# Conditioning loaded by column halves, with eight projection units moved into the second half's loading, in a one-core decoder-layer kernel

## What is computed

```python
mod = (jax.nn.silu(c) @ w_ada + b_ada)[:, None, :]
sh1, sc1, gt1, sh2, sc2, gt2 = jnp.split(mod, N_MOD, axis=-1)
h = rmsnorm(x, g_pre_mix) * (1.0 + sc1) + sh1
m, k_rows, v_rows, s_new = token_mixer(h, w_in, ...)      # proj = h @ w_in, attention, GLA, @ w_out
x = x + gt1 * rmsnorm(m, g_post_mix)
h = rmsnorm(x, g_pre_ffn) * (1.0 + sc2) + sh2
f = (jax.nn.silu(h @ w_ffn_gate) * (h @ w_ffn_up)) @ w_ffn_down
x = x + gt2 * rmsnorm(f, g_post_ffn)
```

## Time and profile before

| what | value |
|---|---|
| time, median of 3 runs | 1493.67 us (1493.54 to 1495.06) |
| profiled execution: time | 1496.05 us |
| profiled execution: span, first to last instruction | 1494.3 us |
| PE busy in the span | 1428.4 us (96%) |
| DVE, ACT busy | 921.6 us (62%), 665.5 us (45%) |
| chain that ended last | PE 83%, DMA 11%, DVE 2%, ACT 2% |
| read from and written to device memory | 382.28 MB, 11.34 MB |

### The profile page before, as it was taken

The page is one execution under the profiler, slowest core; times in us unless marked ns, Lnnn a source line. Parts: engine busy times, 40 slices in busy tenths (PEclk is TensorE's granted clock), DMA queues, the critical chain, the costliest instruction groups (busy, mean ns, idle before and its releaser), DMA issues.

```text
span 1494.3 us, 29193 instructions
## 1 busy us (share of the span) xinstructions
PE 1428.4 (96%) x11238; PEld 1273.0 (85%) x11238; DVE 921.6 (62%) x1519; ACT 665.5 (45%) x1303; POOL 103.8 (7%) x200
## 2 busy tenths in 40 slices
PE   6779999998899999998999999999999999999997
PEld 2247787887667777796899999999999999999997
DVE  2243588995777666368756766567665675446444
ACT  1023477777656454345543434434344343334333
POOL 0000311113322210000000000000000000200000
PEclk9979999999899999999999999999999999999999
DMA  9999999999999979985755565555655555855552
GB/s 370 422 343 364 390 391 405 374 352 391 396 370 343 340 255 356 409 307 225 250 182 183 170 193 173 181 182 170 191 174 181 182 170 192 231 181 181 181 178 95
DMA packets 139330, 396.82 MB, mean 266 GB/s; under 512 B 13162, under 2 KB 17681, under 8 KB 126433
## 3 DMA queue, kind: packets, MB, share of 16 engines
q1 hardware_dynamic: 118018, 319.66, 61.3%
q0 software_dynamic: 21232, 76.10, 13.4%
HBM read 382.28 MB, written 11.34 MB: 263 GB/s over the span
## 4 chain that ended last, share of the span: by engine, by line
PE 83%; DMA 11%; DVE 2%; ACT 2%; issue 1%; POOLq 0%; SPq 0%; POOL 0%; DVEq 0%; ACTq 0%
PE ps L1981 24%; PE ps L1982 24%; PE ps L1983 24%; DMA ada_s<-in_w_ada 5%; PE ps L1915 4%; DMA v_page<-in_cache_v 3%; PE ps L2113 2%; DMA ada_r<-in_w_ada 1%; PE ps L2039 1%; DMA raw<-in_w_ffn_gate 1%; DMA k_page<-in_cache_k 1%; ACT k_page L803 1%; DMA k_page<-in_cache_v 1%; ACT w_hi L715 0%; PE ps L2141 0%
## 5 line engine op out<-in xcount | busy, mean ns | idle before, releaser
L1981 PE MATMUL ps<-h_hi,w_hi 128*128 128x264 f32 x2304 | 667.8, 290 | 11.0 <-DVE h_lo L1249 3.6
L1982 PE MATMUL ps<-h_lo,w_hi 128*128 128x264 f32 x2304 | 659.2, 286 | 0.0
L1983 PE MATMUL ps<-h_hi,w_lo 128*128 128x264 f32 x2304 | 658.6, 286 | 0.0
L1981 PEld LDWEIGHTS ps<-h_hi,w_hi 128*128 128x128 f32 x2304 | 438.9, 190 | 55.8 <-issue 34.9
L1806 DVE TENSOR_TENSOR w_lo<-raw,w_hi 128x1024 fp32r<-128x1024 f32 x254 | 307.2, 1214 | 273.1 <-ACT w_hi L1047 271.7
L1047 ACT ACTIVATE w_hi<-raw 128x1024 fp32r<-128x1024 f32 x264 | 278.5, 1059 | 408.2 <-PE ps L1983 384.4
L1982 PEld LDWEIGHTS ps<-h_lo,w_hi 128*128 128x128 f32 x2304 | 438.2, 190 | 0.5
L1983 PEld LDWEIGHTS ps<-h_hi,w_lo 128*128 128x128 f32 x2304 | 436.9, 190 | 0.0
L1261 DVE TENSOR_TENSOR w_lo<-raw,w_hi 128x1024 fp32r<-128x1024 f32 x138 | 168.7, 1223 | 145.9 <-ACT w_hi L715 145.5
L715 ACT ACTIVATE w_hi<-raw 128x1024 fp32r<-128x1024 f32 x128 | 135.1, 1056 | 172.5 <-PE ps L1983 155.1
L1982 PE MATMUL ps<-act_lo,w_hi 128*128 (+1 forms) x704 | 200.4, 285 | 0.0
(11 more groups left out here) (362 smaller groups left out, 1213.8 us busy)
## 6 DMA issues: line engine op xcount, KB each, us to landing
ada_r<-in_w_ada SPq DMA_DIRECT2D x64, 1024.0 KB, 9.1
raw<-in_w_in SPq DMA_DIRECT2D x96, 512.0 KB, 8.3
raw<-in_w_ffn_gate SPq DMA_DIRECT2D x88, 512.0 KB, 3.5
raw<-in_w_ffn_up SPq DMA_DIRECT2D x88, 512.0 KB, 4.4
raw<-in_w_ffn_down SPq DMA_DIRECT2D x88, 512.0 KB, 4.6
ada_s<-in_w_ada SPq DMA_DIRECT2D x32, 1024.0 KB, 13.7
k_page<-in_cache_k POOLq DMA_DIRECT2D x64, 512.0 KB, 8.0
v_page<-in_cache_v POOLq DMA_DIRECT2D x38, 512.0 KB, 8.4
```

The lines of the kernel that those rows point to most:

```text
L1981: mm(out, w_hi, xh, start=first, stop=False)
L1982: mm(out, w_hi, xl, start=False, stop=False)
L1983: return mm(out, w_lo, xh, start=False, stop=last)
```

## The change

Three things change together.

1. **Columns by halves.** A first step now takes 1024 columns of the shift and the same 1024 of the scale (`ada_halves`), so 16 steps give both for channels 0 to 1023, and 16 more for the rest. `mod_part` and `samples` work on half of the channels.
2. **Units behind steps.** Groups 0 and 1 are cut in two. Their first four units each (the first eight in the order, `unit_of`) need only channels 0 to 1023 and run between the steps of the second half (`UNIT_BEHIND` on PE, `W_BEHIND` on SP). The other four units of each follow as slots 8 to 15; their sums are added by DVE to what ACT copied out (`evac_sum`). The slot programs start at slot 8 (`NSPLIT`).
3. **Steps moved.** n = 0 to 15 now stand in slots 9 to 32, 16 to 23 in slots 34 to 48 (even), and the second half of shift 2 (24 to 31) in slots 97 to 105, with a turn of its own; 32 to 47 in slots 108 to 123. n = 48, 49 and 54 are loaded at the FFN's start. POOL loads the first five K pages before it makes the tree masks. The gate's products move from slots 4, 6, 8 to slots 9, 11, 13.

```diff
-        PARTS = (1, 0, 2, 3, 4, 5)
-        TURN_BANK = (4, 7, 4, 4, 7, 4)
+        PARTS = (0, 0, 2, 3, 3, 4, 5)
+        TURN_BANK = (4, 7, 4, 4, 7, 7, 4)
+        PART_END = (0, 0, 16, 24, 32, 48, 64)
...
+        def unit_of(u):
+            if u < 2 * NSPLIT:
+                half, i = divmod(u, NSPLIT)
+                g, j = divmod(i, UPC // 2)
+                return g, j + half * UPC // 2
+            return divmod(u, UPC)
...
-        A_SLOT = {n: 3 + 9 * n // 8 for n in range(16)}
-        A_SLOT.update({16 + k: 25 + 2 * k for k in range(16)})
-        A_SLOT.update({32 + k: s for k, s in enumerate(
-            (96, 97, 98, 100, 101, 102, 103, 104, 105, 106, 107, 108, 110, 111, 112, 114))})
+        A_SLOT = dict(enumerate((9, 10, 12, 13, 14, 15, 16, 17, 19, 20, 22, 24, 26, 28, 30, 32)))
+        A_SLOT.update({16 + k: 34 + 2 * k for k in range(8)})
+        A_SLOT.update(dict(zip(range(24, 32), (97, 98, 100, 101, 102, 103, 104, 105))))
+        A_SLOT.update({32 + k: 108 + k for k in range(16)})
-        TURN_AT = {20: 2, 55: 3, 115: 4}
+        TURN_AT = {33: 2, 55: 3, 106: 4, 124: 5}
...
+            def ada_halves(n):
                 q, k = divmod(n, KC)
-                return ada_v[:, k, PARTS[q] * 2048:PARTS[q] * 2048 + 2048]
+                return ada_v[:, k, 0:2 * D].rearrange("p (c q i) -> p c q i", c=2, q=2)[:, :, q, :]
...
+            W_BEHIND = {16: 0, 17: 1, 19: 2, 20: 3, 22: 4, 23: 5, 25: 6, 26: 7, 29: 8, 30: 9}
             for n in range(6, 2 * KC):
                 sp.wait_ge(ads_used, n - 5)
-                sp.dma_start(ADS[n % 6][:, :], ada_start(n)).then_inc(ads_in[n % 6], 16)
-            for u in range(4):
-                w_load(u)
+                ada_first_load(n)
+                if n in W_BEHIND:
+                    u = W_BEHIND[n]
+                    if u >= 4:
+                        sp.wait_ge(lo_ready, u - 3)
+                    w_load(u)
...
             mod_row(0)
+            for i in range(3):
+                hi(i)
+                h_high(i)
+            for u in range(3, 7):
+                hi(u)
+            act.wait_ge(ads_used, 14)
+            for m in range(MT):
+                evac(0, m)
+            hi(7)
+            for m in range(MT):
+                evac(1, m)
+            hi(8)
+            hi(9)
             mod_row(1)
-            hi(0)
-            for i in range(NH):
-                h_high(i)
-                if i < 3:
-                    hi(i + 1)
+            h_high(3)
+            hi(10)
+            h_high(4)
...
             mod_part(0)
...
+            samples(0)
+            for i in range(3):
+                prompt(i)
+                lo(i)
+                low(i)
+            for u in range(3, 10):
+                lo(u)
             mod_part(1)
-            dve.wait_ge(mod_done, 2)
-            build_h(0)
+            samples(1)
+            prompt(3)
+            low(3)
+            prompt(4)
+            lo(10)
+            low(4)
+
+            def evac_sum(e, m):
+                if m < 3:
+                    dve.wait_ge(bank_done, 3 * e + m + 1)
+                else:
+                    dve.wait_ge(unit_used, SET_END[e])
+                dve.wait_ge(bank_out, MT * NG)
+                dst = unit_dst(e - NG, m)
+                v.tensor_tensor(dst, dst, ps[:, m, 0:T], ALU.add).then_inc(bank_out, 1)
...
+            UNIT_BEHIND = {18: 0, 19: 1, 20: 2, 22: 3, 23: 4, 25: 5, 26: 6, 28: 7}
+            for n in range(KC, 2 * KC):
+                ada_first(n)
+                if n == KC + 1:
+                    mod_turn(0)
+                if n in UNIT_BEHIND:
+                    unit(UNIT_BEHIND[n])
+            mod_turn(1)
```

More of the change, by code:

```diff
@@ L120, in stickbreak_gla_layer @@
         GLU = put("glu", [P, MT, T], at=r0 + 2 * FC * T * 4)
-        ADS = [put(f"ada_s{i}", [P, 2048], at=r0 + 8192 * i) for i in range(6)]
+        ADS = [put(f"ada_s{i}", [P, 2048], at=r0 + 8192 * i) for i in range(8)]
+        ADS_PLACE = [n % 6 if n < 18 or n % 6 >= 2 else 6 + n % 6 for n in range(2 * KC)]
         MNEG0 = put("mask_neg0", [P, P], at=r0 + 98688)
@@ new lines, in prompt, with low, samples @@
+            def prompt(i):
+                for k in range(*HPC[i]):
+                    ins = v.tensor_scalar(F_LO[:, k, 0:TP], F_LO[:, k, 0:TP], scale_t[:, k, 0:1], MOD[:, k, 0:1], ALU.mult, ALU.add)
+                ins.then_inc(h32_ready, 1)
+            def low(i):
+                cs = slice(*HPC[i])
+                dve.wait_ge(hhi_ready, i + 1)
+                v.tensor_tensor(H_LO[:, cs, :], F_LO[:, cs, :], H_HI[:, cs, :].bitcast(F32), ALU.subtract).then_inc(h_ready, 1)
+            def samples(q):
+                cs = slice(KC // 2 * q, KC // 2 * (q + 1))
+                dve.wait_ge(mod_done, q + 1)
+                link(v.scalar_tensor_tensor(scale_t[:, cs, :], MOD[:, KC + cs.start:KC + cs.stop, :], 1.0,
+                                            vec1[:, NMOD + cs.start:NMOD + cs.stop].unsqueeze(2).to_broadcast([P, KC // 2, NC]),
+                                            ALU.add, ALU.mult))
+                link(v.tensor_tensor(F_LO[:, cs, TP:T], F_LO[:, cs, TP:T], scale_t[:, cs, 1:NC], ALU.mult))
+                v.tensor_tensor(F_LO[:, cs, TP:T], F_LO[:, cs, TP:T], MOD[:, cs, 1:NC], ALU.add)
@@ L1684, in slot @@
                     fold(SQD[:, 12:16, :], MT, acc_ready)
+                if NG <= SET_AT.get(st, 0) < 2 * NG:
+                    for m in range(3):
+                        evac_sum(SET_AT[st], m)
             def gate_scales(gain, part):
@@ L1703, in fold @@
                 ins.then_inc(done, 1)
-            for st in range(NSLOT):
+            for st in range(NSPLIT, NSLOT):
                 slot(st)
@@ L1911, in _, with ada_step @@
             ins.then_inc(tr_done, 1)
-            def ada_step(ring, k, bank):
+            def ada_step(ring, k, bank, first, last):
                 for j in range(4):
-                    ins = mm(ps[32 * j:32 * j + 32, bank, :], CTK[:, k, :], ring[:, j * CG:(j + 1) * CG],
-                             start=(k == 0), stop=(k == KC - 1))
+                    ins = mm(ps[32 * j:32 * j + 32, bank, :], CTK[:, k, :], ring[:, j * CG:(j + 1) * CG], start=first, stop=last)
                 return ins
@@ L1992, in unit @@
                     pe.wait_ge(mix_ready, j + 1)
-                first, last = j == 0, j == UPC - 1
+                first, last = set_of(u - 1) != e, u in SET_AT
                 for m in range(MT):
-                    if first and g > 0:
-                        pe.wait_ge(bank_out, MT * (g - 1) + m + 1)
+                    if first and e > 0:
+                        pe.wait_ge(bank_out, MT * (e - 1) + m + 1)
                     for kk in range(2):
@@ L2226, in _ @@
                     ins.then_inc(g_mm, 1)
-                if st in (6, 8):
+                if st in (11, 13):
                     pe.wait_ge(glow_ready, 1)
                     pe.wait_ge(misc_in, 64)
-                    for h in range(3) if st == 6 else (3,):
+                    for h in range(3) if st == 11 else (3,):
                         if h == 3:
```

281 lines of the change are left out of this document (141 added, 140 removed).

## The result

| | before | after |
|---|---|---|
| time, median of 7 runs | 1495.06 us (1493.54 to 1500.2) | 1500.74 us (1499.12 to 1503.42) |
| profiled execution: span | 1494.3 us | 1498.1 us |

The ratio is 1.0035, 95% interval [1.0019, 1.005]: slower, where 1490 had been forecast and faster was the likeliest sign. The time lies in the range, on rival A's side, but it moved the other way than the forecast.

What follows compares the result with a forecast made beforehand. It took DMA queues to bound the first 437 us, then PE. Terms: -15.3 us by slot 71, +10.1 given back behind slot 97, +1.2 for waits and `evac_sum`, -4.0 in all: 1493.67 becomes 1489.7, predicted 1490, range 1480 to 1501.

Steps and rivals of the forecast that it cites:

- rival A: Slots 20 to 32: bytes loaded there bind, slot 32 ends at 232 to 237 instead of 227; 1499 us, chance 0.20.
- The start: First steps by halves and units 0 to 7 between them: unit 8 starts at 121.4, 1.0 us gained.
- rival D: At the start, first piece of h late, units pile up behind step 31, 10 us lost; 1499 us, chance 0.05.
- Rival B: Units 4 to 7 at 1.2 GHz, unit 8 some 7 us later, 4 us remain; 1494, no change, chance 0.18.
- Slots 20 to 32: PE's bound 225.2, bytes' bound 224.6; slot 32 taken to end at 227, 9.1 us earlier than before.
- Slots 33 to 55: Two steps fewer and one turn more up to slot 55: -1.7 us, to 10.8 early.
- Slots 56 to 71: Slot 55's step and wait go, -2.0; bytes limit the page stretch, smaller backlog gives 2.5; 15.3 us early at slot 71.
- rival C: Page stretch gives more: slots 56 to 71 lose the whole 5.4 us, slot 32 ends at 225; 1485 us, chance 0.15.
- Behind slot 97: Slots 97 to 127: eight steps more, 9.4, and a fifth turn, 0.7, give back 10.1 us; 1.2 more for waits and `evac_sum`.

Runs made afterwards that it cites:

- block: Changed kernel with the first eight units in one block behind step 31, not between the steps of the second half; 1518.24 us, ratio 1.0148.
- q_after: Changed kernel loading only 512 of 2048 columns in the eight steps n = 8 to 15, matmuls kept; ratio 1.0004 to the kernel before.
- spread: Changed kernel with steps n = 8 to 15 in slots 19 to 38, 16 to 23 in 40 to 54, gate 1's turn in 39; ratio 1.0015 to before.
- spread_early: The spread kernel with step 1's data loaded right behind step 0's, before slot 8; ratio 1.0015 to the kernel before.
- evac_first: Changed kernel with ACT's bank copies in slot 31 put ahead of its rounding and K-page sum; ratio 1.0036 to the kernel before.

## Why the prediction was wrong, by its own steps

- **The start: right, and undersized.** Unit 0 began at 67.45 (67.5), so rival D fell. A step of the second half took 2.56 us where nothing stood between the steps (block, 84.42 to 86.98 us), as taken. Unit 4 began at 90.0 behind ACT's copy, as foreseen (92.4), and at full clock: the 3.5 us of waiting there did not lower it. Rival B fell. Unit 8 began at 116.3 (121.4), at 1.2 GHz to 122 as foreseen. With seven steps fewer (8.3 us), 3.0 us were gained by slot 19, not 1.0. But of the 5.1 us by which unit 8 was ahead of the forecast 3.1 were lost again in slots 8 to 19; 2.4 of them are PE's waits for query rows (1.6) and for `evac_sum` (0.8), which the kernel before does not have there.
- **Slots 20 to 32: the step that failed, on rival A's side.** The text put 85.8 MB by slot 32 and 224.6 us by bytes. The trace has 374 GB/s x 232.0 us = 86.8 MB. By 166 us 1.0 MB fewer had been moved (371 against 377 GB/s), since the queues ran empty before step 31 had ended (186 GB/s from 107 to 112 us): 2.5 us. The 1.0 MB more: 2.5. Behind 166 us they moved (86.8 - 61.6) / 66 = 382 GB/s, not 396: 2.4. Together 232. Both bounds "nearly meet", the text said, and took 227, the later one and 1.8 us for all waits. By PE's side, 5.8 us of waits and 2.4 of half clock came on top of its work. The text counted no wait at a group border and no fall of the clock there. q_after, with 6.3 MB less and the same work of PE, took 48.9 us for 56.1, so the steps' bytes are what the term had too small; why full queues moved 382 GB/s and not 396 is not shown. Rival A's sign, PE waits of over 5 us, came; its mark, slot 32 after 232.5, was missed by 0.5. That its total of 1499 lies near the measured one is partly luck: it had slot 32 at 236 and 6.2 us gained from there to slot 71, and measured were 232 and 2.4.
- **Slots 33 to 55: nothing was freed.** Forecast -1.7, measured +0.6. The trace of before showed 0.6 us in the place of the later wait, because a step covered the rest: the wait for the tree in slot 51 (2.4 us) and the clock behind it (0.72 for 6 us) take what the steps gave. The text asked what covers an edit and not what the moved step had covered.
- **Slots 56 to 71: right in kind.** 3.0 us gained (slot 56 1.5, the rest 1.5), forecast 4.5. Over the kernels here this stretch lasts 94 to 98 us whatever stands before it. PE waited 12.1 us for V pages there (11.2 before), not less than 8, so rival C fell.
- **Behind slot 97: right.** 11.6 us given back, forecast 11.3. They fall in slots 113 to 125, where twelve steps stand (two before) with none of PE's time covered. Behind slot 125, in the FFN, 1.3 us came back.
- Sum: -11.3 + 7.2 + 0.6 - 3.0 + 0.0 + 11.6 - 1.3 = +3.8 us, the difference of the spans. The medians differ by 5.7; the other 1.9 us are not in these two executions, and the ledger can't place them.

No version that computes everything beat the kernel before. The nearest are spread and spread_early, 1.0015. In spread 9.7 us are gained by slot 96, and eight steps and a turn more behind it cost 12. What stays open: why slots 20 to 36 of spread and its kin take 70 to 71 us, where the kernel before took 68.3 with the same units and one step and one turn more. It is not that the queues had more to move: they moved 365 GB/s in that stretch of spread and 397 before, while PE stood idle for 6.1 us at a mean clock of 0.95, and before for 4.3 at 1.00. Masks, the pages' table, ACT's order and the number of loads were each tried, and none gives it back.

## What to carry to other kernels

A work item that is moved has two prices: what it costs where it goes, and what it was worth where it stood. Look for a wait of another engine that it covers, and for the bytes that it kept in an otherwise idle stretch; steps in slots 49 to 54 were free, behind slot 112 ten more of them cost 12.0 us. Where PE and the queues are both near their limit in a stretch, as in slots 20 to 32 here, take the later of the two bounds plus the waits at its borders. And look at the issuing queue for the waits of moved loads: one such wait of 10 us was hidden here, and the two experiments that spared PE's time beside it showed no gain.

## What the runs showed of the hardware

- Four matmuls of 32 columns of weights each into the four 32-row groups of a bank run side by side: 1.06 us for four, 1.04 for one. Taking three away spares nothing.
- A wait is followed by half clock or not: 3.6 us before unit 32 by 5.5 us at 0.52, 2.4 us before the tree's turn by 6 us at 0.72, 5.0 us before unit 8 by 5 us at 0.50, the 3.5 us before unit 4 by none. The Trainium skill, TensorE: Matmul & The Clock Gate, "HAM oscillation", tells of a kernel that waits for a DMA between short bursts of matmuls and is throttled again by each wait. Three of the four waits here agree with it in kind, though each is single and ended by ACT or DVE or the building of h and not by a DMA; the fourth brought no fall.
- The releaser that the profile names for a wait on several semaphores can be wrong where it matters: unit 32 waited for ACT's copy (moved ahead in evac_first, it took the wait from 3.6 to 1.1 us), and the profile put it down to DVE in the changed kernel and to ACT in spread.
